# A hybrid attention block in fp32: tables loaded with the output weights, mixed rows transposed one block per retention round

## What is computed

```python
for layer in range(DEPTH):                      # DEPTH = 2
    h = _rms_norm(x, attn_norm[layer])
    (...) = _split_cols(h @ w_in[layer])
    o_diff = _diff_attention(...)               # 512 columns, 4 heads
    o_mla = _mla(...)                           # 256 columns, 4 heads
    o_ret = _retention(r_q, r_k, r_v, r_g, ...) # 256 columns, 4 heads, chunks of 128 tokens
    mixed = jnp.concatenate([o_diff, o_mla, o_ret], axis=-1)
    x = x + mixed @ w_out[layer]
    ...                                         # feed-forward network
```

## Time and profile before

| | us |
|---|---|
| time, median of 3 runs | 2757.05 (2750.95 to 2757.72) |
| the profiled execution's own time | 2758.77 |
| its span, first to last instruction | 2756.9 |
| PE busy | 2596.2 (94%) |
| DVE busy | 1535.2 (56%) |
| ACT busy | 1095.6 (40%) |
| POOL busy | 1010.2 (37%) |
| mean granted TensorE clock | 0.951 of 2.4 GHz |

### The profile page before, as it was taken

How to read it: one execution, slowest core, us unless ns; L and a number is a source line. 1 busy time by engine, 2 the same in 40 slices (tenths; PEclk the granted TensorE clock), 3 DMA queues, 4 the chain that set the end, 5 groups by cost and what they waited for, 6 DMA issues and landing times. The chain is left out here.

```text
span 2756.9 us, 42762 instructions
## 1 busy us (share of the span) xinstructions
PE 2596.2 (94%) x12908; PEld 2227.4 (81%) x12908; DVE 1535.2 (56%) x3045; ACT 1095.6 (40%) x2503; POOL 1010.2 (37%) x1137
## 2 busy tenths in 40 slices
PE   6999988999999999999989998988998999999997
PEld 5999877877778888888879998777886888888886
DVE  4666554462554545477656665544626554445785
ACT  4444544252533222344444445433515222322444
POOL 2455422163154444301044554222712545442012
PEclk9999999959999999999999999998599999999999
DMA  5111011013223333473331101012122332335633
GB/s 175 28 33 44 11 35 37 29 60 107 88 77 110 110 106 108 149 280 96 100 107 31 34 19 39 5 37 73 46 100 71 109 102 88 110 110 211 224 96 122
DMA packets 238648, 242.64 MB, mean 88 GB/s; under 512 B 27904, under 2 KB 171008, under 8 KB 238464
## 3 DMA queue, kind: packets, MB, share of 16 engines
q1 hardware_dynamic: 238464, 240.43, 27.1%
HBM read 172.75 MB, written 67.63 MB: 87 GB/s over the span
## 5 line engine op out<-in xcount | busy, mean ns | idle before, releaser
L2351 POOL TENSOR_TENSOR fw_a_lo<-fw_a_raw,fw_a_hi 128x512 fp32r<-128x512 f32 x132 | 178.6, 1354 | 470.0 <-DVE fw_s_raw L1942 470.0
L2351 POOL TENSOR_TENSOR fw_s_lo<-fw_s_raw,fw_s_hi 128x512 fp32r<-128x512 f32 x176 | 232.0, 1331 | 55.0 <-ACT fw_s_hi L1436 55.0
L722 PE MATMUL banks<-ht_hi,da_hi 128*128 128x512 f32 x496 | 192.9, 389 | 0.0
L722 PE MATMUL banks<-ht_lo,da_hi 128*128 128x512 f32 x496 | 192.9, 389 | 0.0
L722 PE MATMUL banks<-ht_hi,da_lo 128*128 128x512 f32 x496 | 192.9, 389 | 0.0
L722 PE MATMUL banks<-w_diff_hi,ht_hi 128*128 128x384 f32 x512 | 183.1, 358 | 5.9 <-DVE ht_lo L1623 3.9
L722 PE MATMUL banks<-w_diff_lo,ht_hi 128*128 128x384 f32 x512 | 174.7, 341 | 0.0
L722 PE MATMUL banks<-w_diff_hi,ht_lo 128*128 128x384 f32 x512 | 174.5, 341 | 0.0
L2187 POOL TENSOR_TENSOR qk_rot<-rope_a,rope_b 128x512 f32<-128x512 f32 x64 | 82.5, 1290 | 217.4 <-DVE rope_b L1652 217.4
L1680 DVE TENSOR_REDUCE stats<-banks 128x1 f32<-128x1024 f32 (+3 forms) x192 | 138.5, 749 | 32.5 <-PE banks L923 27.5
L722 PE MATMUL banks<-h_t_hi,fw_s_hi 128*128 128x512 f32 x352 | 139.9, 397 | 11.6 <-DVE h_t_lo L1946 8.2
(11 more groups left out here) (350 smaller groups left out, 7571.3 us busy)
## 6 DMA issues: line engine op xcount, KB each, us to landing
da_raw<-act_scratch SPq DMA_DIRECT2D x154, 256.0 KB, 2.7
fw_a_raw<-in_w_gate_dram SPq DMA_DIRECT2D x88, 256.0 KB, 3.1
act_scratch<-act_s SPq DMA_DIRECT2D x66, 256.0 KB, 3.0
w_diff_raw<-in_w_in_dram SPq DMA_DIRECT2D x24, 512.0 KB, 6.2
fw_a<-in_w_up_dram SPq DMA_DIRECT2D x44, 256.0 KB, 3.2
fw_a_raw<-in_w_up_dram SPq DMA_DIRECT2D x44, 256.0 KB, 2.9
act_scratch<-act_zero SPq DMA_DIRECT2D x44, 256.0 KB, 2.4
act_scratch<-act_one SPq DMA_DIRECT2D x44, 256.0 KB, 2.8
```

Source lines behind the costliest of these rows:

```text
L722: mm = pe.matmul(bank, lhsT, rhs, start=first and i == 0, stop=last and i == len(pairs) - 1, skip_group_check=resumes)
L2351: pool.tensor_tensor(w[1][:], w[2][:], w[0][:].bitcast(F32), ALU.subtract).then_inc(S["f_lo"], 1)
```

## The change

SP issues the three small tables right behind `load_out(0)`, inside the MLA loop, in place of waiting for attention's end. For that they get other places in SBUF. The rounding of w_out's first half is put at MLA steps 33 and 34 (parts 0 and 1) and in rounds 0 and 2 (parts 2 and 3), on ACT and POOL. In rounds 5 to 16, PE transposes one block of `mixed_rows` each, behind `ret_inner` and ahead of `ret_output`, into one bank of its own (`Z_BANK`); ACT and DVE evict it at the end of their round. The bank of a retention transpose is now given by the unit's number, and the waits for free banks are written out. The transposes behind the rounds are gone.

```diff
--- before.py
+++ after.py
@@ -280,9 +280,9 @@
     mq_b = sb("mq_b", [P, MLA_HEADS, 2, 16], F32, EREG + 5632)
     m_square = sb("m_square", [P, Q_RANK], F32, MREG + 21 * KB)
 
-    causal = sb("causal", [P, P], F32, EREG)
-    gn_w = sb("gn_w", [P, RET_W], F32, EREG + 2 * KB)
-    gn_b = sb("gn_b", [P, RET_W], F32, EREG + 3 * KB)
+    causal = sb("causal", [P, P], F32, slots[1] + 11 * KB + 512)
+    gn_w = sb("gn_w", [P, RET_W], F32, HT + 62 * KB)
+    gn_b = sb("gn_b", [P, RET_W], F32, HT + 63 * KB)
     rt_hi = [sb(f"rt_hi{i}", [P, 2, P], F32R, HT + (56 + i) * KB) for i in range(3)]
     rt_lo = [sb(f"rt_lo{i}", [P, 2, P], F32R, HT + (59 + i) * KB) for i in range(3)]
     rk_hi = [sb(f"rk_hi{i}", [P, P], F32R, EREG + 10 * KB + 512 * i) for i in range(2)]
@@ -476,14 +476,16 @@
         ROUND_RET = (0, 17)
 
         RET_STEPS = range(RET_UNITS + 8)
-        ROUND_OUT = {0: 0, 2: 1, 4: 2, 6: 3}
+        ROUND_OUT = {0: 2, 2: 3}
 
 
         MIXED_BLOCKS = [(half, k) for half in range(2) for k in range(KD - 2)]
 
+        RET_BASE = RING - NORM2_RINGS - 2 * KD - RET_UNITS
+
         def mixed_blocks(u):
 
-            return MIXED_BLOCKS[2 * (u - RET_UNITS - 2):2 * (u - RET_UNITS - 1)] if u >= RET_UNITS + 2 else []
+            return MIXED_BLOCKS[u - 5:u - 4] if u >= 5 else []
 
 
         FINAL_POOL = 4
@@ -588,11 +590,10 @@
                         if h * T + T - 1 - t == 25:
                             sp.wait_ge(S["z_done"], L * PER["z_done"] + Z_UNITS)
                             load_out(0)
-
-                sp.wait_ge(S["pv_done"], L * PER["pv_done"] + ATT_UNITS)
-                arrives(causal[:], causal_dram, "ret_in")
-                arrives(gn_w[:], ret_gn_w[L].partition_broadcast(P), "ret_in")
-                arrives(gn_b[:], ret_gn_b[L].partition_broadcast(P), "ret_in")
+                            arrives(causal[:], causal_dram, "ret_in")
+                            arrives(gn_w[:], ret_gn_w[L].partition_broadcast(P), "ret_in")
+                            arrives(gn_b[:], ret_gn_b[L].partition_broadcast(P), "ret_in")
+
 
                 sp.wait_ge(S["mix_out0"], L * PER["mix_out0"] + PER["mix_out0"])
                 sp.wait_ge(S["mix_out1"], L * PER["mix_out1"] + PER["mix_out1"])
@@ -979,15 +980,34 @@
                         mla_transpose(a + T)
 
 
+                ret_base = ring[0]
+                assert ret_base == RET_BASE
+
                 def ret_transpose(p, t):
                     n = p * T + t
                     pe.wait_ge(S["rope_sum"], L * PER["rope_sum"] + ROPE_RET + n + 1)
-                    bank = take_ring()
+                    last_use = ret_base - 1 + n if n < 2 else ret_ready[n - 2]
+                    if last_use > freed[0]:
+                        pe.wait_ge(S["tr_free"], L * PER["tr_free"] + last_use)
+                        freed[0] = last_use
+                    ring[0] += 1
+                    bank = banks[:, TR_BANKS[(ret_base + n) % 2], :]
                     pe.transpose(bank[:, tokens(0)], r_rot[n][:, 0:2, :].rearrange("p a d -> p (a d)"), ident[:])
                     pe.transpose(bank[:, tokens(1)], r_rot[n][:, 2:4, :].rearrange("p a d -> p (a d)"), ident[:]).then_inc(S["tr_done"], 1)
                     ret_ready[n] = ring[0]
 
-                ret_ready = {}
+                ret_ready, mixed_ring = {}, [0]
+
+                def mixed_block(half, k):
+                    pe.wait_ge(S["mix_in"], L * PER["mix_in"] + 16)
+                    if mixed_ring[0] > freed[0]:
+                        pe.wait_ge(S["tr_free"], L * PER["tr_free"] + mixed_ring[0])
+                        freed[0] = mixed_ring[0]
+                    ring[0] += 1
+                    mixed_ring[0] = ring[0]
+                    for j in range(4):
+                        tr = pe.transpose(banks[:, Z_BANK, tokens(j)], mixed_rows[:, 4 * half + j, tokens(k)], ident[:])
+                    tr.then_inc(S["tr_done"], 1)
 
                 def ret_inner(p, t):
                     n = p * T + t
@@ -1033,11 +1053,14 @@
 
                 pe.wait_ge(S["s_exp"], L * PER["s_exp"] + PER["s_exp"])
                 pe.wait_ge(S["o_free"], L * PER["o_free"] + PER["o_free"])
+                pe.wait_ge(S["z_free"], L * PER["z_free"] + Z_UNITS)
                 for u in RET_STEPS:
                     if u < RET_UNITS:
                         ret_transpose(u // T, u % T)
                     if 0 <= u - 1 < RET_UNITS:
                         ret_inner((u - 1) // T, (u - 1) % T)
+                    for half, k in mixed_blocks(u):
+                        mixed_block(half, k)
                     if 0 <= u - 2 < RET_UNITS:
                         ret_output((u - 2) // T, (u - 2) % T)
 
@@ -1049,14 +1072,9 @@
                     return [pair for k in blocks for pair in
                             split((ht_hi[:, k, tokens(t)], ht_lo[:, k, tokens(t)]), (w_o[c][0][:, k, :], w_o[c][1][:, k, :]))]
 
-                for half in range(2):
-                    transpose_rows(mixed_rows[:, 4 * half:4 * half + 4, :], "mix_in", 16, range(KD - 2))
-                    if half == 0:
-                        first_half = ring[0]
                 pe.wait_ge(S["r_take"], L * PER["r_take"] + 2 * T)
                 pe.wait_ge(S["w_hi"], L * PER["w_hi"] + PARTS * (CH_OUT + 1))
                 pe.wait_ge(S["w_lo"], L * PER["w_lo"] + CH_OUT + 1)
-                pe.wait_ge(S["tr_free"], L * PER["tr_free"] + first_half)
                 for t in range(4):
                     products(banks[:, t, :], out_pairs(0, t, range(KD - 2)))
                 for half in range(2):
@@ -1359,10 +1377,10 @@
                     return n - n // T
 
                 def ret_high(n):
-                    r = round_ring()
+                    round_ring()
                     if n >= 3:
                         act.wait_ge(S["ro_done"], L * PER["ro_done"] + n - 2)
-                    act.activation(rt_hi[n % 3][:].rearrange("p b n -> p (b n)"), banks[:, TR_BANKS[r % 2], 0:2 * P], ACT.Copy)\
+                    act.activation(rt_hi[n % 3][:].rearrange("p b n -> p (b n)"), banks[:, TR_BANKS[(RET_BASE + n) % 2], 0:2 * P], ACT.Copy)\
                         .then_inc(S["tr_hi"], 1)
 
                 def ret_inner(n):
@@ -1407,6 +1425,7 @@
                     if a > MLA_UNITS:
                         n = a - MLA_UNITS - 1
                         ret_gate_and_v(n)
+                        weights(CH_OUT, [n])
 
                 for u in RET_STEPS:
                     if u < RET_UNITS:
@@ -1421,7 +1440,8 @@
                     if u in ROUND_OUT:
                         weights(CH_OUT, [ROUND_OUT[u]])
                     for half, k in mixed_blocks(u):
-                        high_rows(half, None, [k])
+                        round_ring()
+                        act.activation(ht_hi[:, k, tokens(4 * half, 4)], banks[:, Z_BANK, :], ACT.Copy).then_inc(S["tr_hi"], 1)
                 for half in range(2):
                     high_rows(half, None, range(KD - 2, KD))
                 weights(CH_OUT + 1)
@@ -1832,8 +1852,8 @@
                     return n - n // T
 
                 def ret_low(n):
-                    r = low_ring()
-                    dve.tensor_tensor(rt_lo[n % 3][:].rearrange("p b n -> p (b n)"), banks[:, TR_BANKS[r % 2], 0:2 * P],
+                    low_ring()
+                    dve.tensor_tensor(rt_lo[n % 3][:].rearrange("p b n -> p (b n)"), banks[:, TR_BANKS[(RET_BASE + n) % 2], 0:2 * P],
                                       rt_hi[n % 3][:].rearrange("p b n -> p (b n)").bitcast(F32), ALU.subtract).then_inc(S["tr_free"], 1)
 
                 def ret_inner(n):
@@ -1925,7 +1945,10 @@
                     if 0 <= u - 1 < RET_UNITS:
                         ret_state_low(u - 1)
                     for half, k in mixed_blocks(u):
-                        low_rows(half, None, [k])
+                        low_ring()
+                        at_ = tokens(4 * half, 4)
+                        dve.tensor_tensor(ht_lo[:, k, at_], banks[:, Z_BANK, :], ht_hi[:, k, at_].bitcast(F32), ALU.subtract)\
+                            .then_inc(S["tr_free"], 1)
 
 
                 def gu_sums(m, g, has_before):
@@ -2285,6 +2308,8 @@
                     for p in range(RET_PAIRS):
                         if 0 <= step - ROUND_RET[p] < PARTS:
                             weights(CH_RET + p, [step - ROUND_RET[p]])
+                    if step > MLA_UNITS:
+                        weights(CH_OUT, [step - MLA_UNITS - 1])
 
 
                 def rs_count(n):
```

## The result

| | before | after |
|---|---|---|
| median of 20 runs each, us | 2754.27 (2750.35 to 2757.94) | 2760.73 (2753.71 to 2764.83) |
| ratio after to before | | 1.0022 (95%: 1.0016 to 1.0028) |
| profiled execution, us | 2758.77 | 2764.83 |
| mean granted clock | 0.951 | 0.949 |

The change makes the kernel slower by 6.5 us, 0.22%: within the 8.3 us that I had called no measurable change. Twenty runs resolve it all the same. I had forecast +15.

What follows compares the result with a forecast made beforehand. PE at the 1.2 GHz clock was taken to bound the rounds. Per layer, blocks +12.2 and tail -6.5 gave +5.7; two layers +11.4 plus starts +3.7 made +15.1 us, 2773.9 against 2758.8, range 2757 to 2780.

Steps and rivals of the forecast that it cites:

- POOL takes the place of the stall: First rounds: early roundings on POOL hold output 0 as the table wait did; +2.1 and +1.6 us, 3.7 together.
- the queue: DMA queue at the start: tables ahead of attention's small stores delay POOL's chain by 2 us (1.0 to 3.6).
- The blocks: Rounds 5 to 16: four more transposes each lengthen the round by 1.04 us; 12.2 us a layer (10.0 to 14.9).
- borrowed change of kind: Part of a block's price: 0.27 us for the first pitch and 0.35 for leaving transposes for the next products.
- rival 1: Blocks at 0.86 us, tail gaining 7.4 a layer, starts +0.5 in all: +5.7 us, 2763; chance 0.24.
- The tail: Behind the rounds: of the transposes' 8.87 us, 0.63 stay as the wait for r_take; 8.24 us a layer gained.
- Products at the low clock: First w_out products run at half rate for about 3.7 us; 1.7 us a layer lost (0.8 to 2.5).
- The sum: Whole kernel: +5.7 us a layer, +11.4 for two, plus starts +3.7: +15.1 us, 2773.9.
- rival 4: Delayed stores make the mixed rows land too late, PE waits in round 5; 3 us a layer, 2778; chance 0.06.
- rival 2: The blocks lift the clock to 2.4 GHz from round 5, rounds 4.0 us: 2736; chance 0.08.
- Rival 3: The 3.39 us stall cooled PE; removing it keeps all sixteen rounds at 2.4 GHz: 2733; chance 0.03.
- The rule weighed: Skill page says transposes never engage the full clock; the prediction's trace disagreed, reading 0.98 in 630 to 632, behind the rounds.

Runs made afterwards that it cites:

- tables_only: Kernel before with only the three small tables loaded early, right behind the load of w_out's first half; 2748.04 us against 2753.08 for before.
- rounding_only: Kernel before with only the roundings of w_out's first half moved ahead as in the change; 2753.72 us against 2752.82 for before.
- start_only: Kernel before with the early tables and early roundings, blocks left behind the rounds; 2753.82 us against 2753.08 for before.
- causal_round_late: Kernel before with the causal table alone loaded early, gn_w and gn_b behind the mixed rows, roundings two rounds later; 2742.09 us against 2752.82 for before.
- fill12: causal_round_late with twelve more redundant r_z transposes in each round; 2736.73 us in a single execution, 2742.08 timed against 2751.94 for before.
- double: The changed kernel with each block's four transposes issued twice; 2754.45 us in a single execution.
- fill8: causal_round_late with eight more redundant r_z transposes in each round; 2749.37 us against 2751.97 for before.
- after_fill: The changed kernel with twelve more r_z transposes in rounds 0 to 4 and eight in later ones; 2731.49 us against 2751.94 for before.
- burst: causal_round_late with 24 more transposes in the first retention round alone; 2748.83 us against 2751.97 for before.
- burst_fill4: causal_round_late with 24 more transposes in the first round and four more in each later round; 2767.44 us against 2751.97 for before.
- blocks_fill: causal_round_late with the blocks in rounds 5 to 16, twelve more r_z transposes in rounds 0 to 4, eight later; 2729.65 us against 2751.94 for before.
- block_before_inner: The changed kernel with each block ahead of its round's inner products instead of behind them; 2766.38 us in a single execution.
- causal_early: Kernel before with the causal table alone loaded far earlier, gn_w and gn_b behind the mixed rows; 2743.47 us against 2753.08 for before.

## Why the prediction missed

The direction was right, the size was not: +15 forecast, +6.5 measured. Step by step:

- *POOL takes the place of the stall*: right, in its order and its size. Output 0 comes 2.2 and 1.4 us later; I had 2.1 and 1.6. PE's idle time in rounds 0 and 1 was forecast at 4 us or more and shows as 3.40 and 0.71. tables_only, rounding_only and start_only show that the wait for the table hides most of the roundings' cost, and that the roundings take back the early tables' gain. The bounds of this term, -0.6 and +6, do not follow from my own for the queue: 1.0 and 3.6 in each layer, less the 0.6 of layer 2, give +1.4 and +6.6.
- *The blocks*: the step that failed. I took 1.04 us and it is 0.77; with twelve blocks in two layers that is 6.5 us of the 8.6 us miss. The failing term is the borrowed change of kind, 0.27 and 0.35. The 0.35 is the exit into 64-row products; the block is left for a full-row product, and the 0.27 was the entry behind a 64-row product, while the block stands behind a full-row one. The rows that I needed stood in a round of before, where a full-row product follows another at 0.22, and the block was to stand between these two:

```profile
571.75 0.41 PE L722 MATMUL banks<-rv,rk_lo 128*128 128x128 f32 x1
571.97 0.41 PE L1029 MATMUL banks<-rv,r_at_hi 128*128 128x128 f32 x1
```

My lower bound of 0.86 (4 x 0.21 is 0.84) was also too dear, as the product behind the block starts 0.07 us after its last transpose. The trace of before has that exit too, at the full clock: the product at 635.19, of full rows, starts 0.03 us behind the last of the 48 transposes, whose own pitch there is 0.11. I had the case "everything at its cheap end" as rival 1, at +5.7 us. It came out for this term alone, since the starts cost 3.6 us and not 0.5; that the median lies close to its price is luck.
- *The tail*: -7.96 a layer for -8.24, as the wait for r_sum leaves 1.15 us between the last output and the first product. Right.
- *Products at the low clock*: 1.4 and 2.65 us for 1.7. Right on average (2.0), with the layers apart.
- *The sum*: my terms with the measured sizes give +9.6; the profiled executions differ by 6.1 and the medians by 6.5. Three microseconds outside the stretch, where the diff changes nothing, made the miss larger. Single profiles differ there by as much with the same code, so it may be chance; one profile of each kernel does not settle it.
- *The mixed rows in time* (rival 4): block 0 met no wait in after. Right.
- *The clock* (rival 2): right for this change, 0.50 in every round. But my reason against it, that the rounds' mix keeps 0.50, does not carry: with four more transposes to a block the clock rose. Rival 3, the gap as sole cause, fell: in after and in before PE is full for 60 us behind the gap at 0.50, in before the clock reads 0.50 from 555.0 on, 4.6 us ahead of that gap, and in causal_round_late, where the causal stall is gone and PE has no gap over 0.3 us from 552.8 to 615.6, it is 0.50 over all the rounds as well.
- *The rule weighed*: the Trainium skill, page "TensorE: Matmul & The Clock Gate", section "Part 4: PE-mode transpose", has transposes not count for the full clock. fill12 and double disagree: the only PE work added to a kernel that stays at 0.50 were transposes, and the clock reads 1.00 over the rounds (in double from 607.3 on). By the rule fill12's rounds would last an estimated 4.35 + 12 x 0.21 = 6.9 us at the low clock; they last 3.86.

Of the signs, the round was to be 5.4 us and is 5.12 at 0.50; counted from attention's last transpose output 0 was to come no earlier and comes later, 9.9 us for 9.2 in layer 1 and 9.9 for 9.4 in layer 2; the first w_out product was to start within 0.3 us of the end of the last r_sum and starts 0.33 behind it; the low clock was to last 2 to 5 us over the products and did for 2.9 (636.6 to 639.5) and 5.5 (2002.7 to 2008.2).

What stays open: why a PE without gaps stays at 0.50 over the rounds of before and rises with padding; the runs show that it is so, not what is counted. How long it takes is open too: double, with ten transposes a round, rose 32 us behind its first block in either layer; fill8, with ten a round and once fallen, did not rise in the 21 and 22 us of padded rounds that were left. All padding here was transposes, so whether plain products would do the same was not run. Why the products behind the rounds wait twice as long for the clock in layer 2 as in layer 1 wasn't tried either.

## What to carry over

Take the price of an inserted instruction from the pair of neighbours that it will have, not from the nearest change of kind, and count an exit that another instruction has paid already only once. Two edits that act on the same wait from two engines are to be priced together: here the wait for a table hid most of what the early rounding cost, and the early rounding took back what the early tables gained. Moving the causal table alone was worth nine microseconds, where the early tables with the early rounding were worth nothing. Before moving work into a stage, read the granted clock of both places: the same twelve blocks cost 5 us at 0.50 and gave 12 at 1.00, where they took the place of padding.

## What the runs showed of the hardware

- The granted clock in the retention rounds is 0.50 with PE busy 20.00 of 20.00 us. With eight or twelve transposes more in each round it went to 1.00 ahead of output 0 (fill8 at 556.4, fill12 at 552.8), and in double, whose extra work starts in round 5, only 44 us behind output 0, in both layers. Redundant work on the bound engine so made a stage shorter: the rounds of after_fill take 56.0 us where those of after take 70.4, and the kernel is 27 us faster.
- Once at 1.00, it fell to 0.50 in or up to 1.2 us behind a gap of PE of 0.92 us in burst (562.9), 1.28 in fill8 (590.6) and 1.78 in double (627.8). The length of the gap does not decide by itself: it fell 2.6 us behind a gap of 0.54 in burst_fill4 (568.0) and with only 0.33 us idle in blocks_fill (611.25), and it stayed at 1.00 over gaps of 0.71 in burst (557.0) and 0.82 in layer 2 of after_fill (1908.0).
- At 0.50, four fp32 transposes of 128x128 between full-row products cost 0.77 us (after) and eight 1.63 (double); from the last of a row of transposes to a 64-row product it is 0.35 from start to start in before, after and block_before_inner, and to a full-row product 0.07 in after and double.
- With three small tables, 320 KB in all and two of them broadcasts, issued behind a 2 MB load, gn_w took 7.2 us to land, in place of 3.3, and the stores queued behind them were held up: POOL's wait for a store's buffer ended 10.4 and 10.5 us behind the anchor in after and 9.3 and 9.1 in tables_only, for 8.1 and 8.3 before and 8.3 and 8.2 in causal_early, where none of the tables stands there.
